# Computing the values of the shared keys and values inside the second attention, one pair of heads ahead

## The reference

```python
if layer == N_A_LAYERS - 1:
    k, v = shared_kv(x, g_kv, w_kv)          # after layer 0's last feed-forward
...
m = diff_attention(h, k, v, w_q[j], ..., g_subln[j], w_o[j], lambda_init)   # in layer 1
...
scores = jnp.einsum("bqhcd,bkhcd->bhcqk", qb, k).astype(f32)
p = jax.nn.softmax(jnp.where(causal, scores, -jnp.inf), axis=-1)
a = p[:, :, 0] - lam * p[:, :, 1]
return jnp.einsum("bhqk,bkhe->bqhe", a.astype(v.dtype), v)
```

## Time and profile before

| What | Value |
|---|---|
| median of 3 runs | 2136.25 us (2133.06 to 2136.64) |
| the profiled execution's own time | 2136.16 us |
| its span in the profile | 2134.3 us |
| mean granted TensorE clock | 0.938 of full speed |
| busy: PE, DVE, ACT, POOL | 89%, 60%, 36%, 20% of the span |

### The profile page before, as it was taken

One profiled execution on the slowest core, in us unless ns is written; L12 is line 12 of the kernel. 1 busy time (PEld: TensorE's weight loads), 2 busy tenths in 40 slices (PEclk: granted clock), 3 DMA queues, 4 the chain that ended last, 5 costly groups with the idle time before them and its releaser, 6 DMA issues.

```text
span 2134.3 us, 30642 instructions
## 1 busy us (share of the span) xinstructions
PE 1898.1 (89%) x11270; PEld 1530.4 (72%) x11270; DVE 1286.3 (60%) x2439; ACT 764.9 (36%) x1183; POOL 423.0 (20%) x536
## 2 busy tenths in 40 slices
PE   7999999777788778887799989899989999768998
PEld 7999999733333333333389989899989999668997
DVE  4546955787777777775554556654454445655444
ACT  4346233321221221221144344433444344544433
POOL 4000000276545545455200010000010000110000
PEclk9989999889989989889999999999999999869999
DMA  8324265499999999999765545465545555314552
GB/s 229 100 81 116 60 187 161 156 421 422 421 422 422 421 422 421 422 421 422 311 206 186 187 150 175 152 194 179 193 149 178 178 191 181 99 49 151 191 181 99
DMA packets 231409, 496.65 MB, mean 233 GB/s; under 512 B 21653, under 2 KB 182566, under 8 KB 198566
## 3 DMA queue, kind: packets, MB, share of 16 engines
q1 hardware_dynamic: 188432, 221.36, 33.1%
q0 software_dynamic: 38224, 273.04, 31.0%
q10 hardware_dynamic: 4678, 1.21, 0.3%
HBM read 494.53 MB, written 1.05 MB: 232 GB/s over the span
## 4 chain that ended last, share of the span: by engine, by line
PE 67%; DMA 15%; DVE 7%; issue 4%; POOL 4%; ACT 3%; another core or an unknown queue 0%; DVEq 0%; POOLq 0%; ACTq 0%
PE ps L1759 43%; PE acc L1759 22%; DMA rows_hi<-in_peer_uv,idx_now 13%; POOL raw L614 1%; DMA rows_xh<-in_peer_uv,idx_now 1%; PE acc L1816 1%; POOL rstd L532 1%; POOL arena L614 1%; DVE lo L1106 1%; DVE arena L1486 0%; DVE arena L1482 0%; DVE arena L1489 0%; ACT hi L669 0%; ACT xh L708 0%
## 5 line engine op out<-in xcount | busy, mean ns | idle before, releaser
L1106 DVE TENSOR_TENSOR lo<-raw,hi 128x2048 fp32r<-128x2048 f32 x210 | 479.5, 2284 | 382.3 <-ACT hi L669 382.2
L1759 PE MATMUL ps<-xh,hi 128*128 128x256 f32 x2184 | 626.1, 287 | 7.1 <-DVE xl L1127 5.9
L1759 PE MATMUL ps<-xl,hi 128*128 128x256 f32 x2184 | 622.7, 285 | 0.0
L1759 PE MATMUL ps<-xh,lo 128*128 128x256 f32 x2184 | 622.3, 285 | 0.0
L669 ACT ACTIVATE hi<-raw 128x2048 fp32r<-128x2048 f32 x210 | 400.1, 1906 | 336.7 <-PE ps L1759 276.4
L1759 PEld LDWEIGHTS ps<-xh,hi 128*128 128x128 f32 x2184 | 423.7, 194 | 13.4 <-issue 10.3
L1759 PEld LDWEIGHTS ps<-xl,hi 128*128 128x128 f32 x2184 | 423.7, 194 | 1.5
L1759 PEld LDWEIGHTS ps<-xh,lo 128*128 128x128 f32 x2184 | 423.3, 194 | 0.1
L529 POOL TENSOR_SCALAR ss<-ss 128x1 f32<-128x1 f32 (+2 forms) x34 | 11.6, 342 | 1181.5 <-ACT arena L995 942.0
L1759 PE MATMUL acc<-arena,diag 128*128 128x512 f32 x384 | 189.0, 641 | 48.0 <-ACT diag L941 47.9
L1759 PE MATMUL acc<-rows,diag 128*128 128x512 f32 x192 | 120.7, 794 | 79.5 <-ACT diag L941 63.2
(11 more groups left out here) (279 smaller groups left out, 2853.4 us busy)
## 6 DMA issues: line engine op xcount, KB each, us to landing
raw<-in_w_ffn_gate SPq DMA_DIRECT2D x44, 1024.0 KB, 5.3
raw<-in_w_ffn_up SPq DMA_DIRECT2D x44, 1024.0 KB, 5.3
raw<-in_w_ffn_down SPq DMA_DIRECT2D x44, 1024.0 KB, 5.0
raw<-in_w_in SPq DMA_DIRECT2D x29, 1024.0 KB, 5.5
raw<-in_w_conv_in SPq DMA_DIRECT2D x12, 1024.0 KB, 5.2
raw<-in_w_kv SPq DMA_DIRECT2D x8, 1024.0 KB, 5.4
raw<-in_w_out SPq DMA_DIRECT2D x4, 1024.0 KB, 5.0
raw<-in_peer_w_q SPq DMA_DIRECT2D x4, 1024.0 KB, 5.2
```

Source lines behind the costliest of these rows:

```text
L1106: v.tensor_tensor(lo[s][:, 0:WORDS[p]], raw[s][:, 0:WORDS[p]], hi[s][:, 0:WORDS[p]].bitcast(F32), ALU.subtract).then_inc(lo_done, 1)
L1759: return nc.tensor.matmul(out, l, r, start=first, stop=last)
```

## The change

The kv stage keeps its four key panels. The four value panels become a stage `v` of their own in the plan, behind q, all in bank 3. TensorE multiplies V0 behind the scores of pair 0, and V(i+1) in pair i, between the scores of pair i+1 and the transposes of pair i. ACT evacuates V(i+1) behind the exponentials of pair i+1. ACT and DVE split the panel two further on at the end of each pair: v2, v3, o0 and o1 in pairs 0 to 3. The normed rows for kv go to a place of their own (`kvh`, `kvl`, over the branch outputs `oh`, `ol`), as they are needed until the attention, so `turn("f2")` on ACT waits only for their copies. The outputs of both heads of a pair share bank 2, and `diff_out` of the first head waits for both. `skewed` is no longer used: all four pairs are written out on ACT, DVE and TensorE.

```diff
@@ plan_panels
-    add("kv", 8)
+    add("kv", 4)
     ffn("ffn2")
     add("q", 4)
+    add("v", 4, banks=(3,))
     add("o", 4, banks=())
@@ buffers
+        kvh = oh[:, :, :, :].rearrange("p b k t -> p (b k) t")[:, 4:4 + KD, :]
+        kvl = ol[:, :, :, :].rearrange("p b k t -> p (b k) t")[:, 4:4 + KD, :]
@@ sync
-            for j in range(8):
+            for j in range(4):
                 load(FIRST["kv"] + j, rows_1024(io["w_kv_2"], j * PC))
...
+            for j in range(4):
+                load(FIRST["v"] + j, rows_1024(io["w_kv_2"], D + j * PC))
@@ gpsimd
-            pool.wait_ge(evacuated, EVAC[FIRST["o"]])
+            pool.wait_ge(evacuated, EVAC[FIRST["v"]])
@@ scalar
-                turn(after, xh, after)
+                turn(after, kvh if after == "kv" else xh, after)
...
-            for j in range(8):
+            for j in range(4):
                 p = FIRST["kv"] + j
                 split(p + 2)
-                if j < 4:
-                    evac(p, df_k[:, 2 * j:2 * j + 2, :].rearrange("p h t -> p (h t)"))
-                else:
-                    c = (j - 4) * PC
-                    evac(p, df_v[:, :, c:c + PC], in_=bank(BANK[p]).rearrange("p (t n) -> p t n", t=TT))
-
-            act.wait_ge(panel_used, FIRST["ffn2"])
+                evac(p, df_k[:, 2 * j:2 * j + 2, :].rearrange("p h t -> p (h t)"))
+
+            act.wait_ge(turned_lo, SEND["kv"])
             turn("f2", xh, "f2")
...
+            def evac_v(j):
+                evac(FIRST["v"] + j, df_v[:, :, j * PC:(j + 1) * PC], in_=bank(3).rearrange("p (t n) -> p t n", t=TT))
+
             def diff_out(h, b):
-                act.wait_ge(df_out, h + 1)
+                act.wait_ge(df_out, h - b + 2)
...
@@ diff_pair on ACT
                 if more:
                     for b in range(2):
                         diff_exp(2 * i + 2 + b, b)
+                    evac_v(i + 1)
                 for b in range(2):
                     diff_out(2 * i + b, b)
+                split(FIRST["v"] + i + 2)
 
             for b in range(2):
                 diff_exp(b, b)
-            skewed(act, DIFF_HEADS // 2, diff_pair)
+            evac_v(0)
+            for i in range(DIFF_HEADS // 2):
+                diff_pair(i, i + 1 < DIFF_HEADS // 2)
@@ tensor
             for j in range(4):
-                panel_a(FIRST["kv"] + j, stream=None if j else "kv")
-            for j in range(4, 8):
-                panel_b(FIRST["kv"] + j)
+                panel_a(FIRST["kv"] + j, stream=None if j else "kv", rh=kvh, rl=kvl)
...
+            def values_panel(j):
+                p = FIRST["v"] + j
+                begin(p)
+                pe.wait_ge(evacuated, EVAC[p])
+                for t in range(TT):
+                    last = token_tile(p, t, bank(3)[:, t * PC:(t + 1) * PC], lh=kvh, ll=kvl)
+                last.then_inc(panel_used, 1)
+
             def diff_values(h, b):
                 pe.wait_ge(df_pt_ready, h + 1)
-                wait(pe, df_o_ready, h - 1)
-                out = bank(2 + b)
+                pe.wait_ge(evacuated, EVAC[FIRST["v"]] + h // 2 + 1)
+                wait(pe, df_o_ready, h - b)
+                out = bank(2)[:, TT * b * P:TT * (b + 1) * P]
...
                 if more:
                     for b in range(2):
                         diff_scores(2 * i + 2 + b, b)
+                    values_panel(i + 1)
                 for b in range(2):
                     diff_turn(2 * i + b, b)
...
             for b in range(2):
                 diff_scores(b, b)
-            skewed(pe, DIFF_HEADS // 2, diff_pair)
+            values_panel(0)
+            for i in range(DIFF_HEADS // 2):
+                diff_pair(i, i + 1 < DIFF_HEADS // 2)
```

More of the change, by code:

```diff
@@ L1059, in diff_turned @@
                 nc.scalar.activation(df_pt[b].rearrange("p n t -> p (n t)"), bank(b)[:, 0:3 * P], ACT.Copy).then_inc(df_pt_ready, 1)
+            def evac_v(j):
+                evac(FIRST["v"] + j, df_v[:, :, j * PC:(j + 1) * PC], in_=bank(3).rearrange("p (t n) -> p t n", t=TT))
             def diff_out(h, b):
-                act.wait_ge(df_out, h + 1)
+                act.wait_ge(df_out, h - b + 2)
                 for t in range(TT):
                     wait(act, df_sq, TT * (h - 2) + t + 1)
-                    nc.scalar.activation(sq_dump[:, (TT * b + t) * P:(TT * b + t + 1) * P], bank(2 + b)[:, t * P:(t + 1) * P], ACT.Square,
+                    nc.scalar.activation(sq_dump[:, (TT * b + t) * P:(TT * b + t + 1) * P], bank(2)[:, (TT * b + t) * P:(TT * b + t + 1) * P], ACT.Square,
                                          accum_out=ss[:, NIDX["diff"], bass.ds(h + t * DIFF_HEADS, 1)]).then_inc(df_sq, 1)
-                nc.scalar.activation(df_o[:, :, bass.ds(h * P, P)], bank(2 + b)[:, 0:TT * P].rearrange("p (t e) -> p t e", t=TT),
+                nc.scalar.activation(df_o[:, :, bass.ds(h * P, P)], bank(2)[:, TT * b * P:TT * (b + 1) * P].rearrange("p (t e) -> p t e", t=TT),
                                      ACT.Copy).then_inc(df_o_ready, 1)
@@ L1630, in post @@
                 v.tensor_scalar(xn[:, 1, :], x[:, 1, :], rstd[:, k, 1:2], None, ALU.mult).then_inc(rows_ready[1], 1)
-                turn(after, xh, xl, after)
+                if after == "kv":
+                    turn(after, kvh, kvl, after)
+                else:
+                    turn(after, xh, xl, after)
             ffn(0)
@@ L1737, in _ @@
                 diff_scores(b, b, b * DIFF_SCORE_LINKS)
-            skewed(dve, DIFF_HEADS // 2, diff_pair)
+            for i in range(DIFF_HEADS // 2):
+                diff_pair(i, i + 1 < DIFF_HEADS // 2)
             k = NIDX["diff"]
@@ L1793, in token_tile, with panel_a @@
                 return last
-            def panel_a(p, m=0, i=0, stream=None):
+            def panel_a(p, m=0, i=0, stream=None, rh=xh, rl=xl):
                 begin(p, m, i)
                 for f in range(2):
-                    last = feature_tile(p, f, bank(BANK[p])[:, f * T:(f + 1) * T], stream=None if f else stream)
+                    last = feature_tile(p, f, bank(BANK[p])[:, f * T:(f + 1) * T], rh=rh, rl=rl, stream=None if f else stream)
                 last.then_inc(panel_used, 1)
```

## The result

The change makes the kernel 0.6 to 0.7% slower, by the loop that the prediction named.

The account below looks back on a forecast made before the run. TensorE, busy 89% of the span, was taken to bound the kernel, with DVE setting the attention's rounds. Added terms of 37.9 us less 23.04 gave +14.9, thus 2151.1 us, range 2145 to 2160.

Parts of the forecast that it names:

- the loop that the prediction named: Attention: V(i+1) precedes the transposes DVE's scores need; V(i+2) needs late ACT and DVE splits; rounds of 19 to 21 us.
- kv stage, less: Kv stage: four value panels of 5.76 us each removed, all on the path, 23.04 us shorter.
- (A): Attention start: V0, the scores of pair 1 and V1 come before the first transpose, +5.8 us.
- (B): Attention rounds 1 and 2, with V2 or V3 between: each 21.0 us in place of 9.31 and 9.24, +23.5 us.
- (C): Attention round 3: no V4, but the mix follows DVE's split of o0; 15.05 in place of 8.82 us, +6.2.
- (D): Attention end: the first head's diff_out waits for both heads' values, so one copy is exposed, +0.8 us.
- (E): Behind the attention: DVE's split of o1 stands before the normalising multiplies; 7.5 us in place of 5.9, +1.6.
- R1: Rival, attention: panels fill TensorE's pauses, so the kernel gets faster, -11.4 us, 2124.7 us; chance 0.05.
- R2: Rival, attention: panel delays transposes but its split is early, loop 13.3 us; -5.5 us, 2130.7 us; chance 0.05.
- R3: Rival, attention: V2 and V3 at 1.2 GHz throughout, 10.2 us in place of 7.8; 2155.9 us; chance 0.10.
- The price of the clock: V2 and V3 start at 1.2 GHz for 4.6 us after TensorE's pause, each taking 7.8 us in place of 5.76.

Follow-up runs that it names:

- the runs that open the loop at either place: From the changed kernel: ACT and DVE value splits moved forward, ratio 0.9981; ACT's split alone, 0.9989; value panel moved behind the values on TensorE, 0.9989.
- both moves: Changed kernel with the value panel behind the values, the splits moved forward and DVE's o1 split behind the turn: 2118.6 us, ratio 0.9934; repeated, 2119.4 us.
- a run that went after the 15.2: Kernel with both moves, its value panel moved on TensorE to between the transposes and the values of a pair: 2120.3 us beside 2119.4, ratio 0.994.

## Why the prediction was right

Its steps against the two profiles, each length read the same way in both:

| step | predicted | measured | from |
|---|---|---|---|
| kv stage, less | 23.04 | 23.03 | chain: 46.65 us for 384 matmuls, 23.62 for 192 |
| (A) to the first transposes | +5.8 | +6.7 | 15.03 - 8.33 |
| (B) rounds 1 and 2 | +23.5 | +22.9 | 20.78 + 20.64 - 18.55 |
| (C) round 3 | +6.2 | +6.0 | 14.84 - 8.82 |
| (D) last copy | +0.8 | +0.8 | 6.92 - 6.12 |
| (E) end | +1.6 | +2.1 | 8.07 - 5.93 |
| sum | +14.9 | +15.5 | |

The loop of (B) is in the trace link by link. From the transposes at 1841.29 the links are 0.52, 5.38, 0.89, 0.48, 1.53, 4.32 and 7.66 us, where 0.61, 5.28, 1.0, 0.50, 1.54, 4.33 and 7.8 were taken. The runs that open the loop at either place show that it is the cause and not a neighbour of it. R1 fell: TensorE's idle time in the attention rose. R2 is close to what the run with both splits moved forward became, at 15 instead of 13.3 us. R3 did not happen: V2 took 7.66 us (1854.41 to 1862.07), where 7.8 was taken and 5.8 and 10.2 were the bounds.

The price of the clock came out right for a reason that was in part wrong. The prediction laid the slow start to the pause, as in the earlier trace rows, and let R2 have a pause too short for the clock to fall. The clock fell within 0.2 us of the end of the scores, when the pause had hardly begun, and it fell before V3 without any pause in the run with both splits moved forward. From the starts of V2 and V3 it stayed low for 4.1 and 3.8 us, below the 4.3 that the prediction took for the least; with ACT's split alone moved forward it was some 5.9 and 3.0 us. The full rate was said to be worth 4.0 us in V2 and V3; the run with extra matmuls got back 3.5.

Terms that were mis-sized. In (A) the issue of 16 scores was estimated at 1.3 us: it is 1.6 (1826.26 to 1827.87), twice, and a panel behind scores 5.9. In (E) 7.5 us was taken and 8.07 measured. GpSimd's stretched instruction was not foreseen; it puts off the second factor by some 2 us, and the second multiply waits 1.54 us for it. That this makes the 0.6 us is argued from the trace, no run isolates it. The prediction also held that its rounds contained a gain of 0.5 us a round from writing the loops out; the run that only writes them out gained 0.6 us in all. And of the 15.2 us in which it read TensorE as waiting for DVE, 1.4 us lie ahead of the first scores and are a wait for GpSimd's copies; this changes no term.

What the sum does not hold. The profiled execution of the kernel before lost 2.1 us that no other profile lost: the first 192 matmuls of ffn2 took 24.72 us and the four q panels 24.20, where 23.4 is what these matmuls take in every other profile. Chain rows of the kernel before, of the changed kernel, and of the kernel before with its loop written out, which is the same code there:

```profile
1625.93 24.72 PE ps L1759 x192
```

```profile
1603.50 23.42 PE ps L1772 x192
```

```profile
1626.02 23.43 PE ps L1761 x192
```

So this difference is no gain of the change: the same code takes either time. With it, 15.5 - 2.1 + 0.6 (the changed kernel's profile came later to the kv stage, through stages that it shares) is 14.0 of the 14.2 us between the spans. The medians differ by 11.6 us on the first measurement and by 16.7 on the second. The kernel before ranges from 2130.90 to 2136.75 us over the 21 runs of the second; three of its four first runs lie at the upper end of that. So the base of the prediction, 2136.16, was high by some 3.5 us against the later median of 2132.67. That 2151.1 came within 1 us of the changed kernel's profiled 2150.23 is partly luck; its medians are 2147.89 and 2149.39.

## What to carry to other kernels

Moving work into an engine's idle time works only if it stands, in that engine's order, where it has its operands and nothing urgent stands behind it: ask for each inserted step who waits for the step after it, and do the same for its preparation on the other engines. Here the panel stood ahead of transposes that were ready, and its split at the end of ACT's order; moving both a few lines, and o1's split behind the turn, made 0.65% faster out of 0.6 to 0.7% slower. Here the idle time of TensorE was a sum of short waits before urgent work, and it held a panel only once the order was rebuilt around it. And measure a round on the engine that paces it: with both moves the first transposes came 10.5, 15.2 and 8.8 us apart, while DVE worked through almost without a pause, and a run that went after the 15.2 gained nothing.

## What the hardware did that was not expected

Granted clock. V2 starts at 1.2 GHz behind a TensorE pause of 6.3 us in the changed kernel, and behind one of 0.67 us with the splits moved forward; there V3 starts so with no pause at all. In all three cases 4 to 5 us of score matmuls with small waits between them stood before. By stretch (columns as in the earlier trace rows), those scores and the pause behind them in the changed kernel; then, with the splits moved forward, the scores before V3, the last of them, and the start of V3:

```profile
1843.90:1848.00 4.10, 3.28 (x17) 2.06 (x16) 3.08 (x11) 3.12 (x14) 0.76 (x2) 1.00 0.02 4
1848.30:1854.30 6.00, 0.00 (x0) 0.00 (x0) 2.24 (x2) 3.73 (x12) 0.74 (x2) 0.50 0.00 0
...
1858.20:1861.50 3.30, 2.48 (x14) 1.53 (x13) 3.12 (x12) 2.32 (x11) 0.00 (x0) 1.00 0.01 4
1861.90:1863.00 1.10, 1.05 (x3) 0.33 (x2) 1.06 (x4) 1.10 (x6) 0.00 (x0) 0.50 0.00 0
1863.10:1868.40 5.30, 5.30 (x25) 5.30 (x26) 3.72 (x8) 3.19 (x10) 0.00 (x0) 0.50 0.01 3
```

So in the changed kernel the clock was down for all but the first 0.2 us of the long pause, and before V3 it fell while scores were still running. With 32 matmuls in the pause both panels run at full clock, before V2 because the extra matmuls bore the slow stretch. That stretch cost 1.7 to 1.8 us a panel in the changed kernel and up to 2.6 us elsewhere (V2 with ACT's split alone moved forward: 8.42 us against 5.86). Why the 2 us pause before ffn2 ends in a slow start in one profile of the kernel before and not in another (24.72 against 23.43 us) stays open, and so does what exactly makes the clock fall.

GpSimd beside DVE. A `tensor_scalar` of 128x8 on GpSimd took 2.33 and 2.34 us in two profiles of the changed kernel and 0.20 in the run that moves DVE's split away; in the first it runs from 1906.31 to 1908.64, and DVE's split from 1906.30 to 1908.59:

```profile
1906.30 2.29 DVE L1114 TENSOR_TENSOR lo<-raw,hi 128x2048 fp32r<-128x2048 f32 x1 [7.08 <-ACT hi L674]
```

The Trainium skill ("SBUF — State Buffer", section "Who interferes with whom") says that a DVE instruction with two SBUF inputs contends with a GpSimd instruction that reads SBUF, and that the order of issue decides which of the two is blocked. The trace agrees: DVE's split started 0.01 us ahead of the GpSimd instruction, which ended 0.05 us behind it. The prediction's (E) left this out.
